# A three-layer network on one core: the mixer's output projection, its norm and the routing in another order, the norm applied on columns, and the state-space loop with both sums on TensorE and its output matmuls in turn over four column groups

## The reference, cut to what matters

```python
    mixed = (g_attn * y_attn + g_pool * y_pool) @ w_out[layer]
    x = x + gate1 * mixed
    h2 = rms_norm(x, g_norm2[layer]) * (1.0 + scale2) + shift2
    x = x + gate2 * peer_ffn(h2, w_peer_q[layer], peer_subkeys[layer], peer_u[layer], peer_v[layer])
...
        # peer_ffn, one block of 128 tokens
        q = (hx @ w_q).reshape(TOKEN_BLOCK, PEER_HEADS, 2, PEER_HALF)
        s = jnp.einsum('nhpd,hpkd->nhpk', q, sub_keys).astype(jnp.float32)
        top_s, top_i = lax.top_k(s, PEER_TOPK)
        cand = top_s[:, :, 0, :, None] + top_s[:, :, 1, None, :]
        best_s, best_p = lax.top_k(cand.reshape(TOKEN_BLOCK, PEER_HEADS, PEER_TOPK * PEER_TOPK), PEER_TOPK)
...
        u_sel = u[expert]
        v_sel = v[expert]
        act = jax.nn.gelu(jnp.einsum('nd,ned->ne', hx, u_sel), approximate=False)
        return jnp.einsum('ne,ned->nd', gate * act, v_sel)
```

## Time and profile before

| | us |
|---|---|
| median of 3 runs | 1973.59 |
| lowest and highest | 1970.92, 1974.06 |
| profiled execution, its time | 1973.16 |
| its span in the trace | 1971.3 |

### The profile page before, as it was taken

The page is one execution under the profiler, slowest core; times in us unless marked ns, Lnnn a source line. Parts: engine busy times, 40 slices in busy tenths (PEclk is TensorE's granted clock), DMA queues, the critical chain, the costliest instruction groups (busy, mean ns, idle before and its releaser), DMA issues.

```text
span 1971.3 us, 24987 instructions
## 1 busy us (share of the span) xinstructions
PE 1766.0 (90%) x9500; PEld 1341.8 (68%) x9500; DVE 1456.8 (74%) x2728; ACT 615.8 (31%) x802; POOL 415.5 (21%) x368
## 2 busy tenths in 40 slices
PE   6999888777877878779999898999999999999999
PEld 4788753333333333337999777899989997779998
DVE  7887798888888888868886698665566555867554
ACT  2235320011001100005543312445454544456442
POOL 0011145444544444530000188000000000000000
PEclk9999899998899889999999899999999999999999
DMA  9853599999999999984554421545444454534553
GB/s 394 316 194 129 203 383 421 422 422 421 422 421 421 421 416 412 416 370 170 185 199 171 150 86 65 214 160 188 182 172 178 181 187 158 171 120 156 187 189 117
DMA packets 63854, 502.13 MB, mean 255 GB/s; under 512 B 7200, under 2 KB 7456, under 8 KB 11296
## 3 DMA queue, kind: packets, MB, share of 16 engines
q0 software_dynamic: 37008, 268.98, 33.0%
q1 hardware_dynamic: 25920, 230.45, 31.9%
q10 hardware_dynamic: 848, 1.69, 0.2%
HBM read 500.04 MB, written 1.05 MB: 254 GB/s over the span
## 4 chain that ended last, share of the span: by engine, by line
PE 62%; DMA 17%; DVE 15%; issue 2%; ACT 2%; POOL 1%; SPq 0%; DVEq 0%; ACTq 0%; POOLq 0%
PE PB L897 24%; DMA arena<-in_uv,eidx 14%; PE PB L908 11%; PE PB L879 8%; DVE arena L1651 3%; PE PB L706 2%; PE PB L1051 2%; PE PB L635 2%; DMA ring<-in_uv,eidx 2%; PE PB L844 1%; PE PB L588 1%; PE PB L692 1%; DVE gu_lo L1234 1%; PE PB L985 1%; PE PB L923 1%
## 5 line engine op out<-in xcount | busy, mean ns | idle before, releaser
L879 PE MATMUL PB<-arena 128*128 128x512 f32 x604 | 300.8, 654 | 98.9 <-DVE arena L1662 98.9
L897 PE MATMUL PB<-h_hi,gu_hi 128*128 128x256 f32 x1344 | 376.9, 280 | 0.5 <-DVE gu_lo L1707 0.5
L897 PE MATMUL PB<-h_hi,gu_lo 128*128 128x256 f32 x1344 | 376.9, 280 | 0.0
L897 PE MATMUL PB<-h_lo,gu_hi 128*128 128x256 f32 x1344 | 375.8, 280 | 0.0
L879 PEld LDWEIGHTS PB<-arena 128*128 128x128 f32 x604 | 122.4, 208 | 276.6 <-issue 143.5
L2559 POOL DMA_INDIRECT arena<-in_uv,eidx x193 | 228.7, 1185 | 303.9 <-PE PB L879 201.9
L1651 DVE CUSTOM_DVE_ANT_0 arena<-arena,XN 128x1024 f32<-128x1024 f32 x187 | 223.3, 1222 | 68.0 <-DMA arena<-in_uv,eidx 67.9
L897 PEld LDWEIGHTS PB<-h_hi,gu_hi 128*128 128x128 f32 x1344 | 254.1, 189 | 4.4 <-DVE gu_lo L1707 1.3
L897 PEld LDWEIGHTS PB<-h_lo,gu_hi 128*128 128x128 f32 x1344 | 252.0, 187 | 3.1
L897 PEld LDWEIGHTS PB<-h_hi,gu_lo 128*128 128x128 f32 x1344 | 252.8, 188 | 0.0
L1717 DVE TENSOR_TENSOR act_gs<-PB,XN 128x256 f32<-128x256 f32 x88 | 37.4, 425 | 239.0 <-PE PB L897 238.0
(11 more groups left out here) (433 smaller groups left out, 3070.0 us busy)
## 6 DMA issues: line engine op xcount, KB each, us to landing
ring<-in_ffn SPq DMA_DIRECT2D x88, 1536.0 KB, 6.3
arena<-in_ada SPq DMA_DIRECT2D x24, 768.0 KB, 8.5
ring<-in_qkv SPq DMA_DIRECT2D x12, 1024.0 KB, 4.7
ring<-in_zg SPq DMA_DIRECT2D x8, 1024.0 KB, 5.0
ring<-in_s5b SPq DMA_DIRECT2D x8, 1024.0 KB, 4.8
ring<-in_ada SPq DMA_DIRECT2D x4, 1536.0 KB, 13.7
ring<-in_up SPq DMA_DIRECT2D x4, 1024.0 KB, 5.0
ring<-in_wo SPq DMA_DIRECT2D x4, 1024.0 KB, 5.6
```

The source lines that it names most:

```text
L879: mm = pe.matmul(PB[2 + 2 * t + h][:, :], lhsT=diag(n), rhs=uv[n % UVB][:, 1, h * 512:(h + 1) * 512], start=False, stop=False, skip_group_ ...
L897: mm = pe.matmul(PB[j % 2][:, b * T:(b + 1) * T], lhsT=w[:, j % 2, o:o + P], rhs=h[:, k, :], start=(k == 0 and m == 0), stop=(k == DC - 1 ...
```

## The change

It has three parts.

In the front, `w_out`'s units 2 and 3 are split in halves, DVE's and ACT's `split_up(2)` and the table building `s5_grids` stand later, and the norm is applied in another form: a diagonal matrix of the reciprocal root (`h2_diagonal`, L1619 of the changed kernel) is the right operand of eight matmuls with X (L820) in place of the transposes, scale and shift are turned into columns by 16 small matmuls (`norm2_columns`, L847), and the copies into `hT` multiply and add by column (L1636 on DVE, L2324 ff. on ACT). The row form of h2 for the dot products is written later.

In the order of the routing, PE does `project(0)` between units of `w_out` for tile 1, the queries run in the order QUERIES, the second tile's norm comes behind `route(0)`, the dot products of the first two groups of gathers come ahead of `route(1)`, and `s5_coefs` moves to the end of the gathers. Gather 0 waits for `w_out`'s last unit, gather 7 for `pq` unit 1 in place of 2, and SP loads the first feed-forward unit after two more units are done.

In the state-space loop both differences are matmuls by the identity (the first product is written with its sign turned), `s5_sum(i+2)` stands behind `s5_in(i+3)` and `s5_skip(i)`, the loops over j and m in `s5_out` are exchanged, and iteration 15 has no POOL work: DVE does all four rotations and its scans write in place.

```diff
+        WO_PART = (1, 1, 2, 2, 3, 4, 5, 6)
+        QUERIES = tuple((0, h) for h in range(7)) + tuple((1, h) for h in (2, 3, 4, 5)) + ((0, 7),) + tuple(
+            (1, h) for h in (0, 1, 6, 7))
...
-                pe.wait_ge(h2_ready, t + 1)
+                pe.wait_ge(dg_ready, t + 1)
                 for r in range(2):
                     for j in range(4):
-                        mm = pe.transpose(PB[H2_BANK[t] + r][:, j * P:(j + 1) * P],
-                                          XN[:, t, (4 * r + j) * P:(4 * r + j + 1) * P], ident[:, :])
+                        mm = pe.matmul(PB[H2_BANK[t] + r][:, j * P:(j + 1) * P],
+                                       lhsT=X[:, t, (4 * r + j) * P:(4 * r + j + 1) * P], rhs=dg[:, t, :],
+                                       start=True, stop=True)
...
+            def norm2_columns():
+
+                pe.wait_ge(mix_sum, 8)
+                for j in range(2 * DC):
+                    row, dc = 1 + j // DC, j % DC
+                    mm = pe.matmul(PB[1][:, j:j + 1], lhsT=brow[:, row, dc * P:(dc + 1) * P], rhs=ident[:, 0:1],
+                                   start=True, stop=True)
+                mm.then_inc(ada_full, 1)
...
+            for i in range(4):
+                out_unit(0, i)
+            out_unit(1, 0)
+            norm2_columns()
+            h2_transposes(0)
+            out_unit(1, 1)
+            pe.wait_ge(h1_act, 4)
+            pe.wait_ge(h1_dve, 4)
+            project(0)
+            key_scores(0)
+            out_unit(1, 2)
+            out_unit(1, 3)
+            for m in range(1, NUNIT):
+                if m == 6:
                     h2_transposes(1)
-                pe.wait_ge(h1_act, t + 1)
-                pe.wait_ge(h1_dve, t + 1)
-                for h in range(PH):
-                    m = PH * t + h
-                    project(m)
-                    if m == 0:
-                        key_scores(0)
-                    elif h > 1 or t:
-                        key_scores(m - 1)
+                if m == 7:
+                    pe.wait_ge(h1_act, 8)
+                    pe.wait_ge(h1_dve, 8)
+                project(m)
+                if m > 1:
...
+                    pe.wait_ge(o_ready, i + 1)
+                for m, (c, o) in enumerate(((0, 0), (1, 1), (2, 2), (2, 3))):
+                    for j in range(4):
...
-                pe.wait_ge(turned, i + 1)
-                pe.matmul(bu_bank(i, 0)[:, :], lhsT=ident[:, :], rhs=s5w[:, M_AT[i % 2][0], :, :].rearrange("p j s -> p (j s)"),
-                          start=False, stop=True, skip_group_check=True).then_inc(turn_summed, 1)
+                for b in range(2):
+                    pe.wait_ge(turned, 2 * i + b + 1)
+                    pe.matmul(bu_bank(i, b)[:, :], lhsT=ident[:, :],
+                              rhs=s5w[:, M_AT[i % 2][b], :, :].rearrange("p j s -> p (j s)"),
+                              start=False, stop=True, skip_group_check=True).then_inc(turn_summed, 1)
...
-                if i + 2 < 16:
-                    s5_sum(i + 2)
                 if i + 3 < 16:
                     s5_in(i + 3)
                 s5_skip(i)
+                if i + 2 < 16:
+                    s5_sum(i + 2)
...
-            s5_grids(0)
-            s5_grids(1)
+            split_up(2)
...
-            split_wo(2)
-            s5_grids(2)
-            s5_grids(3)
-            split_wo(3)
-            for step in range(4, 7):
-                s5_grids(step)
+            for i in (2, 3):
+                for h in range(2):
+                    split_wo_half(i, h)
+            s5_grids(0)
+            s5_grids(1)
...
+            def h2_diagonal(t):
+
+                tell(v.tensor_scalar(dg[:, t, :], ident[:, :], stat[:, 6 + t:7 + t], None, ALU.mult), dg_ready)
...
-                tell(v.tensor_copy(hT[:, 4:8, t * P:(t + 1) * P],
-                                   PB[H2_BANK[t] + 1][:, :].rearrange("p (j q) -> p j q", j=4)), h1_dve)
+                for j in range(4):
+                    tell(v.tensor_scalar(hT[:, 4 + j, t * P:(t + 1) * P], PB[H2_BANK[t] + 1][:, j * P:(j + 1) * P],
+                                         ada[:, 4, 4 + j:5 + j], ada[:, 3, 4 + j:5 + j], ALU.mult, ALU.add), h1_dve)
...
             wo_residual(0)
             wo_root(0, (sq0_act, 1), var0_ready, (root0_ready, 1), dve_link)
-            h2_row(0)
+            h2_diagonal(0)
+            keep_columns()
             keep_h2(0)
-            wo_residual(1)
+            for step in range(2, 7):
+                s5_grids(step)
...
             for step in range(4):
                 route(0, step)
+            wo_residual(1)
             wo_root(1, (sq_act, 2), var_ready, (root_ready, 2), rstd_ready)
+            h2_diagonal(1)
+            h2_row(0)
+            keep_h2(1)
             h2_row(1)
-            keep_h2(1)
-            s5_coefs()
+            for g in range(2):
+                dotted(g)
+            for g in range(2):
+                weighed(g)
...
-                    v.tensor_tensor(m1, re, es, ALU.mult)
+                    if i >= 2:
+                        dve.wait_ge(turn_summed, 2 * i - 2)
+                    v.scalar_tensor_tensor(out=m1, in0=re, scalar=-1.0, in1=es, op0=ALU.mult, op1=ALU.mult)
                 elif step == 1:
-                    if i >= 2:
-                        dve.wait_ge(turn_summed, i - 1)
                     v.tensor_tensor(m0, im, es, ALU.mult)
                     note(v.tensor_tensor(re, re, ec, ALU.mult), turned)
                 else:
-                    at["im"] = mark(v.tensor_tensor(im, im, ec, ALU.mult))
-
-            def sum_im(i):
-                im = halves(i)[1]
-                dve.wait_ge(dve_link, at["im"])
-                at["im"] = mark(v.tensor_tensor(im, im, s5w[:, M_AT[i % 2][1], :, :], ALU.subtract))
+                    note(v.tensor_tensor(im, im, ec, ALU.mult), turned)
...
-                    if i + 1 < 16 and b == 0:
-                        sum_im(i + 1)
                 if i == 15:
                     dve.wait_ge(y_full, 14)
                     dve.wait_ge(w_ready, 32)
-                    wr, wi = (s5w[:, W_AT[1] + b, :, :] for b in range(2))
-                    v.tensor_tensor(s5w[:, 10, :, :], wr, es, ALU.mult)
-                    tell(v.tensor_tensor(s5w[:, 11, :, :], wi, ec, ALU.mult), o_dve)
+                    v.tensor_tensor(s5w[:, 8, :, :], re, ec, ALU.mult)
+                    v.tensor_tensor(s5w[:, 9, :, :], im, es, ALU.mult)
+                    v.tensor_tensor(s5w[:, 10, :, :], re, es, ALU.mult)
+                    tell(v.tensor_tensor(s5w[:, 11, :, :], im, ec, ALU.mult), o_dve)
...
+                    elif n == 0:
+                        pool.wait_ge(unit_done, UNIT[("wo", 3)] + 1)
                     elif n == 6:
                         pool.wait_ge(h2_ready, TT)
                     elif n == 7:
-                        pool.wait_ge(unit_done, UNIT[("pq", 2)] + 1)
+                        pool.wait_ge(unit_done, UNIT[("pq", 1)] + 1)
...
-            for i in range(16):
+            for i in range(15):
...
-                if i == 15:
-                    tell(g.tensor_tensor(o[1], wi, es, ALU.mult), o_ready)
-                    continue
```

More of the change, by code:

```diff
@@ L1482, in _ @@
             split_up(1)
-            split_up(2)
             for k in range(3):
```

189 lines of the change are left out of this document (107 added, 82 removed).

## The result

| | before | changed |
|---|---|---|
| median, us | 1973.59 (5 runs, 1970.92 to 1977.65) | 1958.92 (5 runs, 1958.11 to 1962.92) |
| ratio | | 0.9924, 95% interval 0.9909 to 0.9938 |
| span of the profiled execution | 1971.3 | 1957.1 |

By the ratio the change makes the kernel 15.0 us faster (0.0076 of 1973), by the two medians 14.7. The forecast was 1954.9, a gain of 18.3, and the range held the time.

A forecast was written before the change was run, and what follows sets the result against it. The DMA queue was taken to bound the gathers, and PE, with POOL close behind, the state-space loop. 1973.16 less 9.3 (front) and 9.0 (loop) gave 1954.9 us, range 1949 to 1967.

The forecast's parts named there:

- Steps 1 to 5: Front up to the first gather: `route(0)` begins at 211.2, first gather at 223.3, 6.3 us earlier.
- The 3.3: Front, `w_out` in halves: PE's waits for its splits shrink by 3.3 us, bounds 2.0 and 3.4.
- the 1.9: Front, `split_up(2)` moved behind the copies PE waits for: up-projections end 1.9 us earlier, bounds 0 and 2.4.
- step 4: Front, diagonal matmuls to 204.9, copies to 206.3, first query and scores 3.5 us: `route(0)` at 211.2, 6.3 us earlier.
- Steps 6 and 7: Gathers: eighth issued at 241.7, eleventh at 253.8, hardly a hole left in the DMA stream; gain 9.3 us.
- Step 8: Gathers 12 and up: buffers free before they are due, narrowest margin 3.3 us; clock falling at 235 to 245 leaves about 6.
- Steps 9 to 11: State-space loop: first POOL instruction 1.35 us earlier, PE's two sums 1.93, `s5_out` 1.0 with four column groups side by side.
- A: Loop: PE issues no faster than 0.056 us per record, `s5_out` 1.8, loop gains about nothing; 1963.9 us, chance 0.18.
- C: Loop: the exchange in `s5_out` does nothing, 2.39 us, PE's period 6.42, loop +10.5; total 1974.4 us, chance 0.06.
- D: Loop: switching column group at each matmul serialises, `s5_out` 3.5 us, loop +29; total 1993 us, chance 0.05.
- Step 12: Loop: PE's period 5.05 equals POOL's 5.04; POOL's chain -6.6 us, tail behind it -2.4, sum -9.0.
- Rival B: Front gives only 4 to 6 us: clock still falls, or gather 24 or ACT's gelu delays; 1959 us, chance 0.16.

The follow-up runs named there:

- e5: Changed kernel with four matmuls of unused result filling PE's idle time ahead of `s5_out(13)` and `s5_out(14)`; 1958.46 us, ratio 0.9938.
- e11: Changed kernel with `s5_out` in turn over two column groups, then over the other two; 1959.73 us, ratio 0.9928.
- e4: Changed kernel with the old loop order in `s5_out`, one column group after another; 1968.89 us, ratio 0.9981.
- e2: Kernel before with the front part of the change alone; 1967.69 us, ratio 0.9974.
- e6: Changed kernel with six of the next layer's seven matmuls moved ahead of `s5_out(14)`, the seventh behind `s5_out(15)`; 1955.11 us, ratio 0.9914.
- e8: Changed kernel with six next-layer matmuls ahead of `s5_out(14)` and the first query half a unit of `w_out` earlier; 1956.22 us, ratio 0.9918.
- e10: The kernel of e6 run again, beside the changed kernel; 1954.26 us, ratio 0.9900.

## Why the prediction was right, and where it was off

Right in direction, in the two places and in the order of size; the time is 4.0 us above the forecast, 1.9 of it in the front and 2.0 in the loop.

**Steps 1 to 5.** Tile 0's product, forecast at 196.7, is read at 196.36; the diagonal is there at 202.2 (202.8). The 3.3 are measured (PE's stretch of tile 0's product is 11.3 long in place of 14.6, without idle time); for the 1.9 the pair has 2.4, within the 2 us that one execution is worth here. The first query came 0.9 late through the clock, the four copies took 1.93 in place of 1.4 under cover, and `route(0)` begins at 212.3 (211.2). The step to correct is 4: I had looked for the clock only where it was low before. With the clock up, in e5, step 4's distance from the diagonal to the query came out to the tenth (4.63 for 4.6).

**Steps 6 and 7.** PE's wait for the second diagonal is 1.41 (1.4 forecast), the clock is up there. The 2.3 us at the eighth gather are the late `route(0)` (tile 1's residual begins 1.3 late), a residual and a root that took 0.3 more, and 0.8 in the queries behind the diagonal. The sum of the front, -9.3, measured -7.4 in the pair and -7.2 as the difference of the means over three traces of the old front and eleven of the new one; 1.3 of what is missing is the clock's fall ahead of the first query. **Step 8** holds: behind 260 us the queues are full (400 to 426 GB/s in every window up to 870).

**Steps 9 to 11.** All three sizes measured: 1.3 earlier (1.35), both sums 1.9, `s5_out` 1.01 (1.0). Extending two row groups to four column groups was right, and e11 shows the two-group case. Rivals A, C and D fall by this row alone. C's own price was wrong as well, which e4 shows, since e4 is C: I had put its loop 10.5 above the kernel before, it is 3.3 above. I had 15 periods of 6.42 from POOL's first instruction to the last `s5_out` that waits for POOL, 96.3; e4 takes 89.0, as its last iterations have no inputs. A was priced in the same way and was not run; e11, with PE's period of 5.39 above POOL's, lost only 0.9.

**Step 12** is right in its first term and failed in its second. The 6.6 of POOL's chain came as 6.7: `s5_out(14)` begins 88.6 us behind the loop's first matmul in place of 95.3. The tail's -2.4 came as -0.3. I had halved `s5_out` there and kept the clock at 2.4 GHz, but a faster PE waits longer for POOL: 1.81 and 3.52 us in place of 1.44 and 3.04. e5 shows that this costs 2.3 and that it is the clock. Rival B gave 1959, which is the measured time, but not by its way: the front gave 7.4 and not 4 to 6, and the clock stayed up at 235 to 245 us. It was right in kind only, in that the clock fell all the same, at two places that I had not given, ahead of the first query and at the end of the loop.

The Trainium skill's rule, that different tiles work in parallel and only a change of mode drains (TensorEngine Tiling (Array Packing), Key Properties), agrees with 1.01; that no drain was added agrees with inputs that begin 1.01 behind `s5_out`'s first start.

## What to carry to other kernels

Where several engines have nearly equal periods, make the table of all periods before and after each edit: here PE 5.46, DVE 5.2 and POOL 5.04, and the exchange alone gained 2.7, the rest of the loop's change alone lost 3.3, both gained 7.1. Multiply a period only by the iterations that have all of its work, and look whether a carry or a tail gives the slower engine its delay back. When a stage gets shorter on PE, look where PE will wait longer, and put work from behind into that wait; count the wait as a risk to the clock of what follows. To attribute small changes, compare distances between marks and not times from the start, and set the same instructions of two traces against each other.

## What the runs showed of the hardware

Granted clock 1.00: thirty-two records on 32 columns each take 2.39 us one column group after another, 1.47 over two groups in turn and 1.01 over four. In the last case four records start 6 to 7 ns apart, and each column group takes one every 109 ns.

At the end of the new loop, behind 3.06 to 3.52 us of idle time, the clock was at 0.50 in each of six traces; with matmuls in this idle time it was so in none of four, and e5 puts the cost at 2.3 us. But the granted clock is not a function of the idle time just before: behind 3.03 us it fell in e2 and behind 3.04 it didn't in the kernel before, with the same instructions around it. In the three traces in which the loop was 5.5 us shorter (e6, e8, e10) it fell at two places 500 us later, where it fell in no other trace, and cost 2.2 to 2.3 us there.
